# Attention of a two-block network: scores and 128x128 transposes recast as 64x64 tiles in the four quarters of the array

## What is computed

```python
DILATED_PATTERNS = ((128, 1), (512, 4), (2048, 16))   # window, dilation
o, lse = _banded_causal_attention(by_stride(q), by_stride(k), by_stride(v), window // dil)   # per pattern
s = jnp.einsum('bhgnqd,bhgnkd->bhgnqk', q, kb, ...) / math.sqrt(hd)
p = jnp.exp(s - m)
wts = jax.nn.softmax(jnp.stack(lses), axis=0)
o = jnp.sum(wts[..., None] * jnp.stack(outs), axis=0)
o = _rmsnorm(o, attn_norm_gain[l].reshape(ATTN_HEADS, HEAD_DIM))
```

## Time and profile before

| | |
|---|---|
| median of three runs | 3135.67 us |
| lowest and highest | 3131.33 and 3138.91 us |
| profiled execution, own time | 3130.07 us |
| its span, first to last instruction | 3128.2 us |
| TensorE, matmuls | busy 3005.6 us (96%), 23898 records |
| TensorE, weight loads | busy 2484.5 us (79%) |
| VectorE | busy 1733.3 us (55%) |
| ScalarE | busy 1236.0 us (40%) |
| mean granted TensorE clock | 0.992 |

### The profile page before, as it was taken

One profiled execution on the slowest core, in us unless ns is written; L12 is line 12 of the kernel. 1 busy time (PEld: TensorE's weight loads), 2 busy tenths in 40 slices (PEclk: granted clock), 3 DMA queues, 4 the chain that ended last, 5 costly groups with the idle time before them and its releaser, 6 DMA issues.

```text
span 3128.2 us, 56034 instructions
## 1 busy us (share of the span) xinstructions
PE 3005.6 (96%) x23898; PEld 2484.5 (79%) x23898; DVE 1733.3 (55%) x3053; ACT 1236.0 (40%) x2133; POOL 160.1 (5%) x272
## 2 busy tenths in 40 slices
PE   8999999999999999999999999889889999999998
PEld 7898877889878888888777777667667778887886
DVE  7777643365773243435675554655646656666343
ACT  5334434333543221213453432555554434445332
POOL 1011000010000000000000000000002200000000
PEclk9999999999999999999999999999999999999999
DMA  4212132144322111112454422111013322224643
GB/s 147 82 64 94 59 121 82 52 139 156 118 98 74 54 43 59 38 52 86 136 178 157 135 92 96 60 30 33 26 67 130 122 86 83 81 81 154 193 125 121
DMA packets 102168, 297.59 MB, mean 95 GB/s; under 512 B 13296, under 2 KB 13424, under 8 KB 101792
## 3 DMA queue, kind: packets, MB, share of 16 engines
q1 hardware_dynamic: 83648, 237.34, 23.0%
q0 software_dynamic: 12944, 37.32, 3.4%
q10 hardware_dynamic: 5328, 19.34, 1.5%
HBM read 233.88 MB, written 57.94 MB: 93 GB/s over the span
## 4 chain that ended last, share of the span: by engine, by line
PE 80%; DVE 11%; ACT 6%; issue 2%; DMA 0%; POOL 0%; DVEq 0%; SPq 0%; ACTq 0%; POOLq 0%
PE ps L129 65%; PE ps L128 13%; DVE w_lo L168 1%; ACT w_hi L165 1%; PE ps L137 1%; DVE HB L168 1%; DVE HB L178 1%; DVE C L178 1%; DVE a_A L182 1%; ACT m_D L147 1%; DVE m_SS L178 0%; ACT L152 0%; DVE n L178 0%; DVE XLA L168 0%; ACT C L147 0%
## 5 line engine op out<-in xcount | busy, mean ns | idle before, releaser
L168 DVE TENSOR_TENSOR w_lo<-w_raw,w_hi 128x1024 fp32r<-128x1024 f32 (+3 forms) x354 | 373.8, 1056 | 395.9 <-ACT w_hi L165 394.4
L129 PE MATMUL ps<-XHA,w_hi 128*128 128x264 f32 (+3 forms) x1456 | 466.7, 321 | 10.5 <-DVE w_lo L168 5.3
L129 PE MATMUL ps<-XLA,w_hi 128*128 128x264 f32 (+3 forms) x1456 | 457.1, 314 | 0.0
L129 PE MATMUL ps<-XHA,w_lo 128*128 128x264 f32 (+3 forms) x1456 | 455.3, 313 | 0.0
L165 ACT ACTIVATE w_hi<-w_raw 128x1024 fp32r<-128x1024 f32 (+3 forms) x354 | 324.0, 915 | 293.0 <-PE ps L129 210.6
L129 PE MATMUL ps<-XHB,w_hi 128*128 128x512 f32 x920 | 368.0, 400 | 6.9 <-DVE w_lo L168 4.3
L129 PE MATMUL ps<-XLB,w_hi 128*128 128x512 f32 x920 | 358.9, 390 | 0.0
L129 PE MATMUL ps<-XHB,w_lo 128*128 128x512 f32 x920 | 358.8, 390 | 0.0
L129 PEld LDWEIGHTS ps<-XHA,w_hi 128*128 128x128 f32 x1456 | 275.6, 189 | 38.7 <-issue 13.6
L129 PEld LDWEIGHTS ps<-XLA,w_hi 128*128 128x128 f32 x1456 | 275.5, 189 | 21.2 <-issue 3.6
L129 PEld LDWEIGHTS ps<-XHA,w_lo 128*128 128x128 f32 x1456 | 276.0, 190 | 16.5
(11 more groups left out here) (448 smaller groups left out, 5587.8 us busy)
## 6 DMA issues: line engine op xcount, KB each, us to landing
w_raw<-in_f_gate SPq DMA_DIRECT2D x50, 512.0 KB, 3.3
w_raw<-in_f_up SPq DMA_DIRECT2D x50, 512.0 KB, 3.2
w_raw<-in_f_down SPq DMA_DIRECT2D x64, 384.0 KB, 3.2
w_raw<-in_w_out SPq DMA_DIRECT2D x32, 512.0 KB, 3.3
w_raw<-in_w_rkv SPq DMA_DIRECT2D x24, 512.0 KB, 3.4
w_raw<-in_w_attn SPq DMA_DIRECT2D x24, 512.0 KB, 4.1
h<-HB POOLq DMA_DIRECT2D x40, 256.0 KB, 2.5
hid<-C POOLq DMA_DIRECT2D x18, 512.0 KB, 2.9
```

The source lines that it names most:

```text
L129: return Issued(e.matmul(out, a, b, start=start, stop=stop))
L168: return Issued(self.eng and self.eng.tensor_tensor(out, a, b, op))
```

## The change

It concerns attention's TensorE work and the ScalarE copies that follow it.
- The scores of one head become two calls of 64 queries each, so that the two heads and two halves make four calls, each with its own 64x64 quarter of the array. Both halves of a head write the same bank, on its lower and upper partitions.
- A 128x128 transpose, of V and of the weights, becomes four matmuls of 64x64 against the identity, in the order of `SIDES`. Rows 0 to 63 of the source go to one bank, rows 64 to 127 to the other, 64 columns for each block. A unit takes two banks whatever its length, and one event tells when both are filled.
- ScalarE copies each of the two banks with 64 (i + 1) columns, to every second group of 64 columns of `aPT` or `aVT`.
- The five warming matmuls before V are not issued any more.
- Values, squares and everything outside attention stay.

```diff
@@ -2906,10 +2906,15 @@
 UNITS = [(i, h) for i in BLOCKS for h in range(2)]
 
 
+def by_side(a, side, n):
+
+    return a[:, :].rearrange("p (c s x) -> p s c x", s=2, x=64)[:, side, 0:n, :]
+
+
 def attention_load(D, K, j):
     S = K.at
     if j:
-        D.wait_ge(S.pe, ("v", j - 1, 4))
+        D.wait_ge(S.pe, ("v", j - 1))
     D.dma(K.aV[:, :], K.attn[8 + j]).then_inc(K.a_v, ("in", j), by=16)
     if j:
         D.wait_ge(S.pe, ("s", j - 1, 15, 512))
@@ -2929,16 +2934,21 @@
     S, ps = K.at, K.atb
     yield from pause(ATT)
     in3_over(P, K)
+
+    def quarters(banks, src, n):
+
+        for c in range(n):
+            for side, part in SIDES:
+                at = 128 * c + 64 * part
+                op = P.mm(banks[side][heads(part), block(c)], src[heads(side), at:at + 64], K.ident[heads(side), heads(side)], True,
+                          True)
+        return op
+
     for j in range(4):
         yield
-        for c in (0, 4):
-            b = ps.take(P, ("v", j, c))
-            if c == 0:
-                P.warm(b, K, f"v{j}")
-                P.wait_ge(K.a_v, ("in", j))
-            for n in range(4):
-                op = P.tp(b[:, 128 * n:128 * n + 128], K.aV[:, 128 * (c + n):128 * (c + n) + 128], K.ident)
-            op.then_inc(S.pe, ("v", j, c))
+        banks = [ps.take(P, ("v", j, h)) for h in range(2)]
+        P.wait_ge(K.a_v, ("in", j))
+        quarters(banks, K.aV, 8).then_inc(S.pe, ("v", j))
         P.wait_ge(K.a_ld, ("in", j))
         yield
 
@@ -2948,19 +2958,18 @@
             cn = min(512, 128 * (i + 1) - c0)
             if cn > 0:
                 banks = [ps.take(P, ("s", j, u + h, c0)) for h in range(2)]
-                for h in range(2):
-                    P.mm(banks[h][:, 0:cn], K.aq[heads(h), 128 * i:128 * i + 128], K.ak[heads(h), c0:c0 + cn], True,
-                         True).then_inc(S.pe, ("s", j, u + h, c0))
+                for part in range(2):
+                    for h in range(2):
+                        at = 128 * i + 64 * part
+                        op = P.mm(banks[h][heads(part), 0:cn], K.aq[heads(h), at:at + 64], K.ak[heads(h), c0:c0 + cn], True, True)
+                        if part:
+                            op.then_inc(S.pe, ("s", j, u + h, c0))
 
         def turn(u):
             i, h = UNITS[u]
             P.wait_ge(S.act, ("e", j, u))
-            for c0 in range(0, i + 1, 4):
-                b = ps.take(P, ("t", j, u, c0))
-                for c in range(min(4, i + 1 - c0)):
-                    op = P.tp(b[:, 128 * c:128 * c + 128], K.aA[h][:, 128 * (c0 + c):128 * (c0 + c) + 128], K.ident)
-                op.then_inc(S.pe, ("t", j, u, c0))
-            S.pe.at["t", j, u] = S.pe.n
+            banks = [ps.take(P, ("t", j, u, side)) for side in range(2)]
+            quarters(banks, K.aA[h], i + 1).then_inc(S.pe, ("t", j, u))
 
         def values(i):
             b = ps.take(P, ("w", j, i))
@@ -3015,10 +3024,10 @@
         yield
         if j:
             A.wait_ge(S.pe, ("w", j - 1, 7))
-        for c in (0, 4):
-            A.wait_ge(S.pe, ("v", j, c))
-            A.cp(K.aVT[:, 128 * c:128 * c + 512], ps["v", j, c][:, :]).then_inc(a, ("VT", j))
-            ps.done(("v", j, c), a, ("VT", j))
+        A.wait_ge(S.pe, ("v", j))
+        for h in range(2):
+            A.cp(by_side(K.aVT, h, 8), by64(ps["v", j, h][:, :])).then_inc(a, ("VT", j))
+            ps.done(("v", j, h), a, ("VT", j))
         yield
 
         def weights(u):
@@ -3033,11 +3042,10 @@
             i, h = UNITS[u]
             if i:
                 A.wait_ge(S.pe, ("w", j, i - 1))
-            for c0 in range(0, i + 1, 4):
-                cn = min(4, i + 1 - c0)
-                A.wait_ge(S.pe, ("t", j, u, c0))
-                A.cp(K.aPT[h][:, 128 * c0:128 * (c0 + cn)], ps["t", j, u, c0][:, 0:128 * cn]).then_inc(a, ("p", j, u))
-                ps.done(("t", j, u, c0), a, ("p", j, u))
+            A.wait_ge(S.pe, ("t", j, u))
+            for side in range(2):
+                A.cp(by_side(K.aPT[h], side, i + 1), by64(ps["t", j, u, side][:, 0:64 * (i + 1)])).then_inc(a, ("p", j, u))
+                ps.done(("t", j, u, side), a, ("p", j, u))
 
         def values(i):
             A.wait_ge(S.pe, ("w", j, i))
```

## The result

The changed kernel takes 3145.95 us (median of 11 runs, 3144.06 to 3151.06). The kernel before took 3134.89 us in 11 runs beside it. The ratio is 1.0038, 95% interval 1.003 to 1.0046: slower by some 12 us. The forecast was 3128.3 us with a range of 3116 to 3138. The sign was wrong and the range too narrow.

A forecast was written before the change was run, and what follows sets the result against it. TensorE was taken as the bound (80% of the chain). Of 19.8 us saved, 70% is 13.9; less a fifth, 11.1; less 2.7 and 1, -7.4 us on the 3135.7 median: 3128.3 us, range 3116 to 3138.

The forecast's parts named there:

- item 7: Other queues and VectorE's waits: no added cost, with about 2432 more matmuls issued at a rate RWKV's groups already reach.
- Changes of shape: Attention's TensorE timeline: 132 fewer switches of array shape at 0.15 us each, 19.8 us of TensorE time, the largest term.
- Rival E: TensorE's groups: the 0.15 us is not the change of shape and stays at each group's start; -2 to +3, chance 0.07.
- Turns: Transposes of weights and V: 320 blocks, each four calls and eight records, 0.008 us more each, +2.5 us.
- The group of rows 5: RWKV's r_BK in the profile before: 64 records, eight blocks, 0.93 us without entering, taken as 0.117 us a block.
- Scores: Attention's 48 score pairs in quarters: about 0.05 us saved per pair, 2.4 us.
- Rival C: Score calls: four quarters don't run at once at 512 columns or with shared rows; +14, 3150 us, chance 0.04.
- ScalarE's copies: ScalarE's copies of turned weights: 15.7 us of later ends, 17% on the chain, +2.7 us, from 0 to 15.7.
- Banks: PSUM ring: turns below block 4 take two of four banks, so scores wait for copies; bound 0 to +3 us.
- The clock: Removed warming before V's first turn: no time by itself, but falls to 1.2 GHz cost +1 us, from 0 to 5.
- ScalarE (B): Values and scores: two full copies behind the whole turn stand in their path, making it slower, 3144 us; chance 0.10.
- rival A: Attention's stretch: TensorE's gain is mostly eaten by waits, a quarter of 19.8 arrives; about -1.5, 3134 us, chance 0.24.

The follow-up runs named there:

- e1_warm: The changed kernel with the five warming matmuls ahead of V's first turn put back; ratio 1.0041 to the kernel before.
- e2_scores: The kernel before with the scores alone in 64x64 quarters, turns still transposes and the warming kept; ratio 0.9999 to the kernel before.
- the second warming: Five more warming matmuls behind V's first transposes, on the kernel before with scores alone in quarters; ratio 0.9986, repeat 0.9988.
- f3_act: The kernel before with ScalarE's copies of turned weights as many and as late as in the changed kernel, TensorE's matmuls untouched; ratio 1.0007.
- f1_half: The changed kernel with the warming back and half the calls per turn, each twice as wide, result not the reference's; ratio 1.0009 to the kernel before.
- e4_nowarm: The kernel before without the five warming matmuls, nothing else changed; ratio 1.0018.

## Why the prediction was wrong

**The step that failed** is in item 7: "About 2432 more matmuls with as many weight loads are issued, at a rate that RWKV's groups already reach." They were costed at nothing. RWKV's groups do reach that rate, 64 records in 0.93 us, but over the whole stretch TensorE ran at less than a third of it (40 instructions per microsecond for 138), and the rate at which instructions arrive was never asked. Before, 7613 records and as many loads in 376.6 us are 59 packets of 256, one in 6.3 us; after, 78 packets in 389.3 us, one in 5.0 us, and 3.7 from 2144 to 2174 us, with 3.33 as the least. A turn now lies beside RWKV's groups of the same density, and the two together use up what has arrived. The price, by the starved time, is 14 to 15.5 us; by the idle time at a block's edge alone it is 9 to 13. The profile of before had both halves of it: the page's line of q8, and TensorE's waits for "issue" among the waits.

The Trainium skill (Runtime: NRT & Kernel Launch, Instruction fetch mechanics) says that instructions come in blocks of 16 KiB, 256 of them, and that crossing a block is mostly hidden. The first half agrees with q8's 3.41 MB in 208 packets. The second doesn't hold here where 64x64 matmuls stand close: 18 stops at a block's edge in the stretch, 10.5 us, the longest 1.1 us.

**The sum of e1_warm**, which has before's warming, in the same kind of accounting: starved +15.5 us; waits for the other engines and DMA +3.0; half of the time worked at 1.2 GHz +1.4; what is left, TensorE's own work, -8.8. Together +11.1, and the stretch is 11.0 longer. Point by point:

1. Changes of shape: 132 forecast to go, 133 went (234 to 101). In an undisturbed place the 0.06 of entering is there (1.00 us for eight blocks). But items 1 to 3 together were to take 19.7 us off TensorE's own work, and 8.8 came, so this term, the largest, was too big as well. The missing 11 I can't place: RWKV's groups give 6.5 and the scores 3.5, and the turns rise by 1.5. Delays too short to be told from the usual distance, by the same shortage, would look like this; no run shows it apart. Nor is its size firm: a second count of the same kind, with late starts taken only at a block's edge, gives 10.6 us of the 19.7 in e1_warm, 15 in the changed kernel and 7.5 of 9.9 in e2_scores, and moves with how the time at 1.2 GHz is charged. The cleanest bound is in times: the scores alone (50 changes and item 3, 9.9 us of TensorE, of which 56% were to arrive, 5.5 us) gave at most 3 us by e2_scores and 4 with the second warming. Rival E, that the 0.15 us is not all a change of shape's, is the nearest of the rivals to this and stays open.
2. Turns: 0.124 us a block with the change of shape in it, as forecast, where nothing stops them. The group of rows 5 was right on the array's side; what it left out was the supply.
3. Scores: right, 0.91 us for four calls of 512. Rival C falls with it: four quarters do run at once, as the four calls take what two took before.
4. ScalarE's copies: f3_act gives 2 us for 2.7 forecast. Widths behaved: 592 ns for 512 columns, 286 for 128. ScalarE's waits for TensorE before these copies grew from 13.3 to 21.5 us and were covered nearly whole.
5. Banks: no wait of its own was found; f1_half, which keeps the two banks and all the copies, is only 0.09% above before.
6. The clock: "no time by themselves" for the warming matmuls held only for idle time. Removing them costs 0.18% in the kernel before, over the bound of 5 us by a little. "One more fall at most here" was low: the clock was at 1.2 GHz for 3.4 us from 1967.9 before and for 17 us from 1960 after. The sign "if falls of the clock multiply" came true with it, but putting the warming back brought the clock back and no time. That a TensorE which waits for instructions anyway loses less by a slower clock would explain it; no run shows that.
7. The failed step, above.

The sign that the prediction named for its failure, "if the stretch is no shorter while groups are", is what happened. None of the rivals had this mechanism: the slower ones were ScalarE (B), refuted by f3_act and f1_half, and the quarters (C), refuted by the timeline. The forecast's other signs (fewer than 110 changes of shape, busy time down by 10 us) were met and told nothing of the time. One sum of the prediction is off without weight: rival A's terms give -1.3 and not -1.5.

## What to carry to other kernels

Before a few large TensorE calls are replaced by many small ones, count instructions, with the weight loads, by stretch, divide by 256 and hold the distance of packets against the closest at which the packets of that queue start in the trace: here 3.33 us, and 3.27 in the closest pair of all fourteen kernels. By an estimate from this, a stretch that wants more than about 77 TensorE instructions per microsecond has to stop. In practice the pace was lower: where TensorE stopped at two blocks in a row, 32 of 33 such pairs were 3.4 to 4.3 us apart, 60 to 75 instructions per microsecond. A stop of "issue" in the middle of a group of equal calls is the sign, and its proof is that the stops lie a multiple of 256 instructions apart. Take the part of such a change that adds few instructions (here the scores: 192 records for 50 changes of shape) and leave the part that adds many (the turns: 2240 for the rest).

## What was not expected of the hardware

- TensorE's instructions come in packets of 16 KB, never closer than 3.33 us in the kernel after and 3.38 in the kernel before, and it goes on 1.2 to 1.6 us after a packet's end. Before the change it stops at a block's edge 3 times in attention, so the limit was touched already.
- A change of shape measured at 0.15 us in single places did not add up: 131 fewer changes gave some 9 to 11 us in e1_warm, together with the +2.5 and -2.4 of items 2 and 3, where 19.7 were counted.
- The clock fell for 17 us where TensorE waited for V and for a_k with no warming in between (2.08 and 1.58 us in the timeline above), against 3.4 us before. The missing warming alone does not make it so long: e4_nowarm has the same two waits (1.89 and 1.90 us) and was at 1.2 GHz for 6.8 and 3.4 us there. Five more warming matmuls gave a time clear of the kernel before only together with the scores in quarters.
